# Shifting the token chunk borders to 364, 728 and 1088, and starting four streamed tensors 8 bytes into their rows

## The chip, the cores and the metric

The kernel runs on one core of one Trainium2 chip. The metric is the device time of one execution in microseconds. Before the change, three runs gave 1800.13, 1801.63 and 1802.25 us, a median of 1801.63 us. Five engines work side by side: PE (TensorE, the matmuls, with PEld for its weight loads), DVE (VectorE), ACT (ScalarE), POOL (GpSimd) and SP (SyncE, which only issues transfers).

## The reference, cut to what matters

One step of a small encoder: 1024 prompt rows and 64 sample rows of width 1024. The kernel treats them as T = 1088 tokens side by side. Layer by layer it computes

```python
h   = rmsnorm(x, g_norm1) * (1 + sc1) + sh1
z   = h @ w_in                                  # 1024 x 2464
mix = concat(mla(z), retention(z), stick_breaking(z)) @ w_o    # 1024 x 1024
x   = x + g1 * mix
h   = rmsnorm(x, g_norm2) * (1 + sc2) + sh2
a, b = split(h @ w_up)                          # 1024 x 5632, two branches of 2816
y   = (silu(causal_conv3(a)) * b) @ w_down      # 2816 x 1024
x   = x + g2 * y
out = rmsnorm(x, g_final)
```

All is float32. The sample's caches enter the attention part, which this change leaves alone.

## The kernel before, in words

The work is one program with one instruction stream for each engine, written out by hand; semaphores order the streams. The stages follow each other: transposes and the first norm, the projection `w_in` (line 1748), the mixers, then the late stages, which are what the change touches.

In the late stages the tokens lie along the free axis: a tensor `[128, KT, T]` holds 1024 features as KT = 8 rows of 128 partitions and T = 1088 tokens in each row, 4352 bytes a row. The tokens are cut into three chunks by `CHUNKS`. Chunk 0 is columns 0 to 363 (364 wide), chunk 1 columns 364 to 725 and chunk 2 columns 726 to 1087 (362 wide each).

Every large product of these stages is done in three matmuls: an operand is split into a rounded float32r part (`hi`) and the rest (`lo`), and weight_hi x hi, weight_lo x hi and weight_hi x lo are added in PSUM. The weights are the stationary side, the activations the streamed (moving) side. The streamed tensors are `a_hi` and `a_lo` (named `act_hi` and `act_lo` in the profile, 8 rows each) and `u_hi` and `u_lo` (2 rows each, one for even and one for odd tiles).

- `project(out, c, slot)` (line 1965) streams chunk c of all eight rows: 24 matmuls in a row into one PSUM bank. It serves the output projection `w_o` (24 pairs of feature tile d and chunk c, in the order of `PROJ`, each followed by one float32 matmul of line 1973 that sums squares) and both branches of `w_up`.
- `down(f, slot, ring, tile_no, n)` (line 2024) does `w_down` for one hidden tile f: 24 pieces q, each of three matmuls (u_hi, u_hi, u_lo), where q goes over d = q // 3 and c = q % 3. A part n is four pieces, 12 matmuls.
- `up(...)` makes one hidden tile of the MLP: for n = 0 to 5 it calls `project` for chunk n % 3 and branch n // 3 and then `down` part n of the tile before. There are 22 hidden tiles. `very_first` is another order for the first tile alone (both branches of a chunk one after the other, no `down`).

So one hidden tile is 6 x 24 + 72 = 216 matmuls. Each `project` and each piece of `down` waits on semaphores of ACT and DVE that empty the PSUM banks and write the streamed tensors: ACT writes `a_hi` and `u_hi` (line 1177), DVE writes `a_lo` and `u_lo` (line 1611) and adds PSUM into the residual (lines 1556 and 1620).

`NORM_RUNS` cuts the columns for the two norms; its second half is `CHUNKS`, its first half is for the early norm. `spare` is a tensor that nothing uses: its size `FF_SPARE` keeps the tensors behind it, the weights `wt_raw` and `wt_parts` first, from overlapping `mix_raw`.

Each tensor begins at a multiple of 32 bytes in its partition (in the kernel before `u_hi` at 19488, `u_lo` at 28192, `act_hi` at 115808, `act_lo` at 150624, `wt_parts` at 66656). A row of 4352 bytes is 272 times 16 bytes, so where a chunk begins within 16 bytes is the same in each row of all four tensors: chunk 0 at 0, chunk 1 (column 364, byte 1456) at 0, chunk 2 (column 726, byte 2904) at 8.

Of the kernel before, what the change touches and what calls it, by code (L numbers as in the profile page):

```python
# [15 lines left out]
F32R = mybir.dt.float32r  # L16
# [6 lines left out]
KT = D // P  # L23
LP, LS = 1024, 64
T = LP + LS
PAST = 512
NTILE = 9
ROWS = [P] * 8 + [LS]
CHUNKS = [(0, 364), (364, 726), (726, 1088)]
CW = 364  # L30
H_MLA, NOPE, ROPE, HV = 8, 64, 32, 64
QD = NOPE + ROPE
# [7 lines left out]
NF = FF // P  # L40
# [3 lines left out]
N_TAB = 11  # L44
AG = 512

NORM_RUNS = ([(0, 128), (128, 364), (364, 726), (726, 1088)], CHUNKS)
NH = (0, KT * 4)
ADA_A, ADA_G = 4, 12
MLA_SCALE = float(QD) ** -0.5  # L50
# [3 lines left out]
def segments(c):  # L54

    return split_run(*CHUNKS[c])

# [4 lines left out]

def chunk_of(t, runs=CHUNKS):

# [67 lines left out]
KINDS = [("S", 0), ("M", 0), ("M", 1), ("S", 1), ("M", 2), ("M", 3), ("S", 2), ("M", 4), ("M", 5), ("S", 3),  # L132
         ("M", 6), ("M", 7)]
UNITS = [(n, kind, h) for n in range(NTILE) for kind, h in KINDS]
FF_SPARE = KT * T - (4 * T + 2 * (T + 4) + T + 2 + 2 * CW + 8 + 4 * NF + 9)
T_LAG = {"M": 2, "S": 5}
EARLY_SPLIT = 103
MIX_STEP = 17
# [84 lines left out]
def build(nc, I, O, stop_after=None):  # L223
# [5 lines left out]
    with ctx:  # L229
# [117 lines left out]
        s4 = sbuf(late)  # L347
# [1 line left out]
        mix_scope = ExitStack()  # L349
        mix_raw = sbuf(mix_scope)("mix_raw", [KT, T])  # L350
        mix_scope.close()
        u_hi = s4("u_hi", [2, T], F32R)
        u_lo = s4("u_lo", [2, T], F32R)
        a_ext = s4("a_ext", [2, T + 4])
        conv = s4("conv", [T + 2])
        u_val = s4("u_val", [2, CW])
# [4 lines left out]
        wt_raw = s4("wt_raw", [RAW_SLOTS, KT * P])  # L361
        wt_parts = s4("wt_parts", [WT_SLOTS, 2, KT * P], F32R)
        wt_hi, wt_lo = wt_parts[:, :, 0, :], wt_parts[:, :, 1, :]
        a_hi = s4("act_hi", [KT, T], F32R)
        a_lo = s4("act_lo", [KT, T], F32R)
        res = s4("residual", [KT, T])
        late.close()

# [445 lines left out]
        def _(act):  # L814
# [36 lines left out]
            def square(c, k, j):  # L851

                a, b = CHUNKS[c]
                if j >= 2:
# [3 lines left out]
            def rstd(c):  # L858

                a, b = CHUNKS[c]  # L860
                out = norm_bufs[1]["rb"][:, a:b]
# [5 lines left out]
            def h_high(n, c):  # L867
                for k in range(KT):
                    j = NH[n] + 8 * c + k
                    act.wait_ge(s_hn, j + 1)  # L870
                    base = NORM_RUNS[n][c][0]
                    for a, b, which in split_run(*NORM_RUNS[n][c]):
                        last = act.activation(norm_bufs[n]["hi"][:, k, a:b],
# [55 lines left out]
            split_w_in(0, 0)  # L929
            for c in range(len(NORM_RUNS[0])):  # L930
                h_high(0, c)
# [190 lines left out]
            pieces_done(act, ORDER[-1])  # L1122
            for c, (lo, hi) in enumerate(CHUNKS):
                for k in (0, 4):
# [93 lines left out]
        def _(dve):  # L1218
# [73 lines left out]
            def normed(n, c, k):  # L1292
                bufs = norm_bufs[n]
                j = NH[n] + 8 * c + k
                if k == 0:
                    dve.wait_ge(s_rb, 3 * n + next(i for i, x in enumerate(CHUNKS) if NORM_RUNS[n][c][1] <= x[1]) + 1)
                if j >= 3:
                    dve.wait_ge(s_h, j - 2)
                base = NORM_RUNS[n][c][0]
                for a, b, which in split_run(*NORM_RUNS[n][c]):  # L1300
# [777 lines left out]
```

## Time and profile before

| what | value |
|---|---|
| median of three runs | 1801.63 us (1800.13 to 1802.25) |
| span of the profiled execution | 1796.0 us |
| PE busy / PEld busy | 94% / 84% of the span |
| DVE / ACT / POOL busy | 59% / 36% / 9% |
| mean granted TensorE clock | 0.963 of full |

The profile lists one time for its execution, the span from the first to the last instruction; the median of the runs is 5.6 us above it (0.3%), which is what lies around the span. The busy time of PE counts matmuls that overlap, and their ends are modelled, so a busy PE is not a PE at its peak: how long a matmul really holds the engine is read from a stretch that holds a known number of them, as its length divided by that number. This is called the pitch below.

### The profile page before, as it was taken

To read this page: it belongs to the slowest core of one execution; us is meant where nothing else is said; L and a number is where in the kernel's file an instruction comes from. 1 tells how busy PE (TensorE), PEld (TensorE's weight loads), DVE (VectorE), ACT (ScalarE), POOL (GpSimd) and SP (SyncE) were. 2 spreads that over 40 slices of the span, in tenths; PEclk is the share of its full clock that TensorE was granted. 3 is DMA by queue.
4 is the path that set the end of the run, shared out by engine and by line. 5 is a ranking of instruction groups with operands and counts; after the bars stand their busy time and mean duration, and the time that the engine had idled before them with its cause. 6 is when DMAs were issued, how large, how long until landed. Compare 5 with 4: busy or idle time off the path is not lost.

```text
span 1796.0 us, 27961 instructions
## 1 busy us (share of the span) xinstructions
PE 1680.7 (94%) x10081; PEld 1505.3 (84%) x10081; DVE 1061.4 (59%) x2259; ACT 644.5 (36%) x1242; POOL 164.6 (9%) x220
## 2 busy tenths in 40 slices
PE   6699999979789999999899899999999999999996
PEld 4499999835566677777898899999999999999996
DVE  4853333247777766766424676666656565666657
ACT  6531211125555665667413422122212222212213
POOL 0011111122322221311000000000000000000000
PEclk8799999988888899999999999999999999999999
DMA  7564444431121101005410111111111111111002
GB/s 246 179 223 153 130 131 147 126 121 36 44 88 46 46 13 46 16 1 172 151 44 12 48 48 36 59 35 47 37 56 42 40 48 46 47 35 58 12 0 113
DMA packets 114423, 133.63 MB, mean 74 GB/s; under 512 B 15003, under 2 KB 91722, under 8 KB 113002
## 3 DMA queue, kind: packets, MB, share of 16 engines
q1 hardware_dynamic: 110953, 121.83, 21.5%
q0 software_dynamic: 3328, 10.73, 1.7%
q8 instruction: 46, 0.75, 0.2%
q14 instruction: 32, 0.25, 0.0%
q10 hardware_dynamic: 64, 0.07, 0.0%
HBM read 107.54 MB, written 27.29 MB: 75 GB/s over the span
## 4 chain that ended last, share of the span: by engine, by line
PE 84%; DVE 7%; ACT 4%; issue 3%; DMA 1%; SPq 0%; DVEq 0%; ACTq 0%; POOLq 0%
PE psum L1965 33%; PE psum L2024 15%; PE psum L1748 13%; PE psum L1936 5%; PE psum L1889 3%; PE psum L1918 2%; PE psum L1833 2%; PE psum L1893 2%; PE psum L1787 1%; PE psum L1782 1%; PE psum L1814 1%; PE psum L1683 1%; PE psum L1684 1%; DVE h_lo L1313 1%; PE psum L1973 1%
## 5 line engine op out<-in xcount | busy, mean ns | idle before, releaser
L1965 PE MATMUL psum<-act_hi,wt_parts 128*128 128x362 f32 (+1 forms) x2496 | 620.1, 330 | 13.3 <-DVE act_lo L1548 5.7
L1965 PEld LDWEIGHTS psum<-act_hi,wt_parts 128*128 128x128 f32 x2496 | 442.7, 189 | 19.7 <-issue 10.7
L1620 DVE SCALAR_TENSOR_TENSOR residual<-psum,mod,residual 128x364 f32<-128x364 f32 (+2 forms) x704 | 299.9, 494 | 257.7 <-PE psum L2024 257.5
L1965 PE MATMUL psum<-act_lo,wt_parts 128*128 128x362 f32 (+1 forms) x1248 | 408.8, 328 | 0.0
L2024 PE MATMUL psum<-u_hi,wt_parts 128*128 128x362 f32 (+1 forms) x1056 | 263.3, 331 | 3.0 <-issue 3.0
L1965 PEld LDWEIGHTS psum<-act_lo,wt_parts 128*128 128x128 f32 x1248 | 235.7, 189 | 0.0
L1748 PE MATMUL psum<-w_hi,h_hi 128*128 128x308 f32 (+1 forms) x576 | 178.0, 309 | 14.1 <-DVE h_lo L1313 13.0
L2024 PEld LDWEIGHTS psum<-u_hi,wt_parts 128*128 128x128 f32 x1056 | 188.1, 189 | 3.3 <-issue 3.3
L1748 PE MATMUL psum<-w_lo,h_hi 128*128 128x308 f32 (+1 forms) x576 | 177.3, 308 | 0.0
L1748 PE MATMUL psum<-w_hi,h_lo 128*128 128x308 f32 (+1 forms) x576 | 176.8, 307 | 0.0
L2024 PE MATMUL psum<-u_lo,wt_parts 128*128 128x364 f32 (+1 forms) x528 | 174.8, 331 | 0.0
L1177 ACT ACTIVATE u_hi<-u_val 128x362 fp32r<-128x362 f32 (+1 forms) x66 | 33.4, 507 | 291.0 <-DVE u_val L1603 291.0
L1340 DVE COPY z_out<-psum 128x308 f32<-128x308 f32 (+1 forms) x72 | 34.3, 477 | 161.2 <-PE psum L1748 156.2
L1748 PEld LDWEIGHTS psum<-w_hi,h_hi 128*128 128x128 f32 (+1 forms) x576 | 107.1, 186 | 20.0 <-issue 8.8
L1156 ACT ACTIVATE a_ext<-psum 128x364 f32<-128x364 f32 (+1 forms) x88 | 32.1, 392 | 225.0 <-PE psum L1965 225.0
L1748 PEld LDWEIGHTS psum<-w_lo,h_hi 128*128 128x128 f32 (+1 forms) x576 | 107.1, 186 | 2.2
L1748 PEld LDWEIGHTS psum<-w_hi,h_lo 128*128 128x128 f32 (+1 forms) x576 | 106.8, 185 | 0.4
L1080 ACT ACTIVATE pT<-psum 128x512 f32<-128x512 f32 (+3 forms) x156 | 69.2, 475 | 100.0 <-PE psum L1918 99.9
L1936 PEld LDWEIGHTS psum<-v_mla,pT 128*128 128x128 f32 (+1 forms) x656 | 82.9, 195 | 25.5 <-issue 8.6
L1523 DVE TENSOR_TENSOR wt_parts<-wt_raw,wt_parts 128x1024 fp32r<-128x1024 f32 x74 | 91.0, 1232 | 21.6 <-ACT wt_parts L1101 21.6
L2024 PEld LDWEIGHTS psum<-u_lo,wt_parts 128*128 128x128 f32 x528 | 100.4, 190 | 0.0
L1936 PE MATMUL psum<-v_mla,pT 128*128 128x64 f32 (+1 forms) x656 | 84.6, 276 | 5.4 <-DVE mixtok L1518 2.8
(215 smaller groups left out, 2287.9 us busy)
## 6 DMA issues: line engine op xcount, KB each, us to landing
ada_raw<-in_w_ada SPq DMA_DIRECT2D x48, 512.0 KB, 4.3
wt_raw<-in_w_up SPq DMA_DIRECT2D x44, 512.0 KB, 3.8
wt_raw<-in_w_down SPq DMA_DIRECT2D x22, 512.0 KB, 4.4
w_raw<-in_w_in SPq DMA_DIRECT2D x16, 616.0 KB, 7.1
z_scratch<-z_out POOLq DMA_DIRECT2D x64, 154.0 KB, 2.3
z_in<-z_scratch SPq DMA_DIRECT2D x8, 1232.0 KB, 5.3
xT_scratch<-xT SPq DMA_DIRECT2D x1, 4352.0 KB, 16.3
residual<-xT_scratch SPq DMA_DIRECT2D x1, 4352.0 KB, 14.3
```

What stands on the lines that cost most here:

```text
L1080: last = act.activation(pT[:, wn % 4, :len(blocks), :r], src[:, :len(blocks), :r], ACT.Copy)\
L1340: dve.tensor_copy(z_out[:ROWS[t], t % 3, :], bank[t % 3][:ROWS[t], 0:ZG]).then_inc(s_zc, 1)
L1523: dve.tensor_tensor(wt_lo[:, slot], wt_raw[:, raw], wt_hi[:, slot].bitcast(F32), ALU.subtract)\
L1620: last = dve.scalar_tensor_tensor(out=res[:, d, a:b], in0=bank[4 + q % 4][:, a - CHUNKS[c][0]:b - CHUNKS[c][0]], scalar=mod[:, 40 + d, whi ...
L1748: last = pe.matmul(bank[t % 3][:r, 0:ZG], hh[:, k, P * t:P * t + r], ww[:, slot, k, :], start=(k == 0 and m == 0), stop=(k == KT - 1 and m ...
L1833: last = pe.matmul(b7[:r, 0:384], qnT[:, k, :r], w_uq[:, k, 384 * (s - 2):384 * (s - 1)], start=(k == 0), stop=(k == 2))
L1889: last = pe.matmul(out, qT[:QD, slot, h, :r], kT[:QD, h, first + a:first + b], start=True, stop=True)
L1893: last = pe.matmul(out, sqT[lo:lo + 64, slot, h // 2, :r], skT[lo:lo + 64, h // 2, first + a:first + b], start=True, stop=True)
L1918: last = pe.transpose(out[:size, P * k:P * k + r], src[:, col - first:col - first + size], ident[:r, :r])
L1936: last = pe.matmul(bank[6][:r, 64 * (v % 8):64 * (v % 8) + 64], pT[:size, W_NO[x] % 4, k % 4, :r], vals, start=(k == 0), stop=(k == len(bl ...
L1965: last = pe.matmul(out[:, :b - a], ww[:, slot, P * k:P * k + P], aa[:, k, a:b], start=(k == 0 and m == 0), stop=(k == KT - 1 and m == 2))
L2024: last = pe.matmul(bank[4 + q % 4][:, :b - a], ww[:, ring, P * d:P * d + P], uu[:, slot, a:b], start=(m == 0), stop=(m == 2))
```

## The change

The border between chunk 1 and chunk 2 goes from column 726 to 728, so the chunks are 364, 364 and 360 wide; the early norm's cut moves with it. The four streamed tensors get 8 more elements at their end, and their data begin at element 2 of what is allocated. `FF_SPARE` shrinks by 16 elements, so `wt_raw`, `wt_parts` and `act_hi` stay where they were.

```diff
-CHUNKS = [(0, 364), (364, 726), (726, 1088)]
+CHUNKS = [(0, 364), (364, 728), (728, 1088)]
...
-NORM_RUNS = ([(0, 128), (128, 364), (364, 726), (726, 1088)], CHUNKS)
+NORM_RUNS = ([(0, 128), (128, 364), (364, 728), (728, 1088)], CHUNKS)
...
-FF_SPARE = KT * T - (4 * T + 2 * (T + 4) + T + 2 + 2 * CW + 8 + 4 * NF + 9)
+OFF = 2
+FF_SPARE = KT * T - (4 * T + 16 + 2 * (T + 4) + T + 2 + 2 * CW + 8 + 4 * NF + 9)
...
-        u_hi = s4("u_hi", [2, T], F32R)
-        u_lo = s4("u_lo", [2, T], F32R)
+        def off_line(name, rows):
+            whole = s4(name, [rows * T + 8], F32R)
+            return whole[:, OFF:OFF + rows * T].rearrange("p (a n) -> p a n", a=rows)
+
+        u_hi = off_line("u_hi", 2)
+        u_lo = off_line("u_lo", 2)
...
-        a_hi = s4("act_hi", [KT, T], F32R)
-        a_lo = s4("act_lo", [KT, T], F32R)
+        a_hi = off_line("act_hi", KT)
+        a_lo = off_line("act_lo", KT)
```

After the change each chunk of each of the four tensors begins 8 bytes past a multiple of 16: columns 0, 364 and 728 are bytes 0, 1456 and 2912, all multiples of 16, and 8 is added. Nothing else of the program is edited: the instructions, their order and their semaphores are the same.

## Rows read from the trace of the kernel before

**Rows 1.** The page: busy time of PE, and the chain that ended last

```profile
PE 1680.7 (94%) x10081; PEld 1505.3 (84%) x10081; DVE 1061.4 (59%) x2259; ACT 644.5 (36%) x1242; POOL 164.6 (9%) x220
...
PE 84%; DVE 7%; ACT 4%; issue 3%; DMA 1%; SPq 0%; DVEq 0%; ACTq 0%; POOLq 0%
PE psum L1965 33%; PE psum L2024 15%; PE psum L1748 13%; PE psum L1936 5%; PE psum L1889 3%; PE psum L1918 2%; PE psum L1833 2%; PE psum L1893 2%; PE psum L1787 1%; PE psum L1782 1%; PE psum L1814 1%; PE psum L1683 1%; PE psum L1684 1%; DVE h_lo L1313 1%; PE psum L1973 1%
```

**Rows 2.** Stretches of the late stages, all engines (columns in the first line)

```profile
core 0: us, PE busy (x) PEld busy (x) DVE busy (x) ACT busy (x) POOL busy (x), PEclk, DMA share, GB/s
865.00:986.40 121.40, 119.78 (x672) 113.61 (x672) 46.82 (x74) 34.18 (x55) 0.00 (x0) 0.99 0.19 61
986.40:1022.17 35.77, 29.75 (x169) 29.49 (x169) 22.93 (x57) 19.26 (x36) 0.00 (x0) 0.95 0.19 55
1022.17:1757.00 734.83, 734.83 (x4455) 734.83 (x4455) 464.61 (x991) 165.24 (x244) 0.00 (x0) 1.00 0.13 40
```

**Rows 3.** Stretches, L1965 alone: five calls of project on chunk 0, MLP

```profile
1063.76:1067.75 4.00, 4.00 (x24) 3.85 (x24) 1.00 0.00 0
...
sum 19.98, PE 19.98 PEld 19.27; mean PE 4.00 PEld 3.85
```

**Rows 4.** Stretches, L1965 alone: five calls of project on chunk 1, MLP

```profile
1069.76:1073.72 3.96, 3.96 (x24) 3.81 (x24) 1.00 0.46 132
...
sum 19.79, PE 19.79 PEld 19.07; mean PE 3.96 PEld 3.81
```

**Rows 5.** Stretches, L1965 alone: five calls of project on chunk 2, MLP

```profile
1075.73:1079.57 3.85, 3.85 (x24) 3.72 (x24) 1.00 0.00 0
...
sum 19.23, PE 19.23 PEld 18.58; mean PE 3.85 PEld 3.72
```

**Rows 6.** A stretch, L1748 alone: 48 matmuls of the input projection, 308 wide

```profile
258.37:265.17 6.80, 6.80 (x48) 6.71 (x47) 1.00 0.41 123
```

**Rows 7.** A stretch, L1965 alone: chunk 2, both branches of the first hidden tile

```profile
1002.13:1010.21 8.07, 8.07 (x48) 8.07 (x49) 1.00 0.22 67
```

**Rows 8.** Stretches, L1965 alone: chunks 0, 1 and 2 in the output projection

```profile
892.61:896.89 4.28, 4.28 (x24) 4.02 (x24) 1.00 0.00 0
897.23:901.46 4.24, 4.24 (x24) 3.99 (x24) 1.00 0.43 123
901.79:905.99 4.20, 4.20 (x24) 3.95 (x24) 1.00 0.00 0
```

**Rows 9.** Stretches, L2024 alone: four pieces of chunk 0 in those parts

```profile
1085.57:1086.07 0.50, 0.50 (x3) 0.50 (x4) 1.00 0.00 0
...
sum 2.00, PE 2.00 PEld 1.85; mean PE 0.50 PEld 0.46
```

**Rows 10.** Stretches, L2024 alone: four pieces of chunk 2 in those parts

```profile
1086.57:1087.08 0.51, 0.51 (x4) 0.51 (x4) 1.00 0.00 0
...
sum 2.02, PE 2.02 PEld 1.88; mean PE 0.51 PEld 0.47
```

**Rows 11.** Stretches, L2024 alone: three parts of down, twelve matmuls each

```profile
1085.57:1087.58 2.01, 2.01 (x12) 1.86 (x12) 1.00 0.01 2
...
sum 6.02, PE 6.02 PEld 5.58; mean PE 2.01 PEld 1.86
```

**Rows 12.** The instructions that write u_lo on DVE and u_hi on ACT

```profile
L1611 DVE TENSOR_TENSOR u_lo<-u_val,u_hi x66: 526/530/539, 1013.4 to 1761.3; 128x362 fp32r<-128x362 f32 x44, 128x364 fp32r<-128x364 f32 x22
L1177 ACT ACTIVATE u_hi<-u_val x66: 505/507/510, 1012.9 to 1760.8; 128x362 fp32r<-128x362 f32 x44, 128x364 fp32r<-128x364 f32 x22
```

**Rows 13.** Groups by line and shape, 1022 to 1757 us (busy us, mean ns | idle before)

```profile
L1620 DVE SCALAR_TENSOR_TENSOR residual<-psum,mod,residual 128x364 f32<-128x364 f32 x167 | 98.3, 589 | 6.3 <-PE psum L2024 6.3
L1620 DVE SCALAR_TENSOR_TENSOR residual<-psum,mod,residual 128x362 f32<-128x362 f32 x167 | 98.2, 588 | 119.6 <-PE psum L2024 119.6
```

## Prediction

> **What bounds the kernel now.** I read the page's busy times and chain first. PE is busy for 94% of the span and holds 84% of the chain; the two lines of the late products, L1965 and L2024, alone hold 33% and 15% of it [rows 1]. Then the stretches by stage: from 1022 to 1757 us PE is busy in all of 734.83 us, at granted clock 1.00 (2.4 GHz), while DVE is busy 464.61 us and ACT 165.24 us [rows 2]. No engine makes PE wait there, so this stretch is as long as 4455 matmuls times their pitch, 734.83 / 4455 = 164.9 ns. The output projection before it is nearly the same: 119.78 of 121.40 us [rows 2]. Only between 986 and 1022 us does PE lose 6 us to other engines (the second norm).
>
> The reader's next question is what sets the pitch, and for that I cut the stretch by chunk. 24 matmuls of `project` are followed to the start of the next line, five times each. Chunk 0 takes 19.98 us / 120 = 166.5 ns [rows 3], chunk 1 19.79 / 120 = 164.9 ns [rows 4], chunk 2 19.23 / 120 = 160.3 ns [rows 5]. What a column costs comes from the input projection, whose 308-wide streams take 6.80 us / 48 = 141.7 ns [rows 6]: 56 columns fewer than chunk 0 and 24.8 ns less, 0.44 ns a column, so two columns are 0.9 ns. Chunks 1 and 2 have the same width and differ by 4.6 ns; what tells them apart in the code is where they start: chunk 1 at a multiple of 16 bytes, chunk 2 at 8 past one. So far it looks as if a start at 8 saved some 5 ns.
>
> Three rows spoil this picture. In the first hidden tile the same chunk 2 with the same start takes 8.07 us / 48 = 168.1 ns, of which a slow first matmul after a wait is only a small part [rows 7]. In the output projection chunk 2 is only 0.04 us in 24 (1.7 ns a matmul) better than chunk 1 and 0.08 us (3.3 ns) better than chunk 0 [rows 8]. In `down` chunk 2 is no better at all: twelve matmuls take 2.02 us, 168.3 ns, against 2.00 us, 166.7 ns, for chunk 0, which is wider [rows 9, 10]. The start at 8 thus permits the short pitch but doesn't guarantee it; it holds while equal streams follow each other in long rows.
>
> **The change part by part.** Every estimate is a difference of pitches times a count. 22 hidden tiles x 2 branches x 24 = 1056 `project` matmuls a chunk; `w_o` has 8 calls a chunk; `down` 22 x 72 = 1584 matmuls. The sum is made against the profiled span, 1796.0 us, and carried to the median of the runs, 5.6 us above it, unchanged.
>
> *The MLP's project, chunks 0 and 1 (364 wide, start 0 becomes 8).* Best end: chunk 2's 160.3 ns and two columns more, 161.2 ns: 5.3 and 3.7 ns gained, 1056 x 9.0 = 9.5 us. Least end that still has an effect: what the start is worth in the output projection, 3.3 ns against chunk 0 less 0.9 ns of width, so 166.5 - 2.4 = 164.1 ns. I take the middle, 162.6 ns, because [rows 3 to 5] and [rows 8] show the same two starts in two surroundings and nothing says which the new streams will be nearer: 3.9 and 2.3 ns, 4.1 + 2.4 = 6.5 us gained. The other end, a loss, is that chunk 1 takes chunk 0's pitch with its width: 1.6 x 1056 = 1.7 us.
>
> *Chunk 2 (362 becomes 360 wide, still at 8).* Two columns, 0.9 ns x 1056 = 1.0 us gained, if it keeps its short pitch. If it falls back to what it had in the first tile, near 166.5 ns, it loses 6.2 x 1056 = 6.5 us; that is the upper end.
>
> *The output projection.* Chunks 0 and 1 to about 4.22 us (chunk 2's 4.20 and two columns in 24 matmuls), chunk 2 to 4.18: 0.06, 0.02 and 0.02 us x 8 = 0.8 us gained; at worst 0.04 and 0.08 us lost on chunks 1 and 2, 1.0 us.
>
> *`down`.* Now 6.02 us / 36 = 167.2 ns [rows 11]; the widths' sum stays 1088. Best end: chunk 2's 160.3 ns for the mean width, 160.6 ns, 6.6 x 1584 = 10.5 us gained, because all streams would now start alike, where before each third piece differed. Worst end: chunks 0 and 1 as chunk 2 is now, 1.6 ns x 1056 = 1.7 us lost. I take 0, the value nearest to [rows 9, 10], where the start at 8 shows no gain in threes.
>
> *The writers and readers.* ACT and DVE write the shifted tensors with starts at 8; chunk 2 was written so before, and the 66 instructions of each kind lie within 505 to 510 and 526 to 539 ns [rows 12]. DVE's adds take 589 ns at 364 and 588 ns at 362 columns [rows 13]. Both engines have over a third of the stretch free, which hides a few ns; without that cover, the roughly 30 instructions a tile would cost some 0.1 us a tile. No wait, instruction, queue or transfer is added. A faster PE asks more of DVE: 464.61 us of work in perhaps 715 us is still no bound. The early norm and the second norm get two columns more in one chunk and two fewer in the next: nothing.
>
> Sum: 6.5 + 1.0 + 0.8 + 0 = 8.3 us. Span 1787.7 us, and the median 1793.3 us.
>
> Here a rule is weighed. The rows above show that pitch isn't a matter of width alone. The Trainium skill, "TensorE: Matmul & The Clock Gate", section "Back-to-back issue gap", gives N / 2.4 + 2.5 ns between warm matmuls, a figure in which no address stands. By it the change, which keeps 1088 columns, would be worth 0 us. Chunks 1 and 2 differ by 4.6 ns at one width, so this trace does not agree with it.
>
> **The rivals.**
>
> *All streams lock at the short pitch, `down` too.* 9.5 + 1.0 + 0.8 + 10.5 = 21.8 us: 1779.8 us. For it: chunk 2 has its short pitch in each of the five calls cut, one like the other [rows 5]; after the change no stream has another start. Against it: [rows 7, 10]. Chance 0.15.
>
> *The pitch goes by width and history, and the start is chance.* Chunk 1 becomes 364 wide and takes chunk 0's 166.5 ns: 1.7 us and 0.3 us (output projection) lost; chunk 2 gains 1.1 us; the rest stays. 1802.5 us, no change to be seen. The same comes out if the shift does nothing. For it: two columns more go with 1.6 ns more from chunk 1 to chunk 0. Against it: chunk 2 against chunk 1. Chance 0.25.
>
> *A stream pays by the 16-byte lines that it touches.* A 364-wide stream from 8 covers 92 of them instead of 91; chunk 2 keeps 91. If a line costs what its four columns do, 1.8 ns, then 2 x (1056 + 192 + 528) = 3552 matmuls lose 6.4 us: 1808.0 us. Against it: before the change all three chunks cover 91 lines, and their pitches lie 6.2 ns apart [rows 3, 5]. Chance 0.04. The Trainium skill, "SBUF — State Buffer", section "Specifications (TRN2)", names lines of 16 bytes and a penalty for each crossing to a new one; this trace shows no such penalty at an uneven start.
>
> *Slower: chunk 2 loses its short pitch.* The place is `project` on chunk 2. Before, hi and lo streams lay a multiple of 64 bytes apart; the 8 extra elements put `act_lo` 32 bytes further, so the third matmul of each three now starts elsewhere within 64 bytes than the two before it, and the even sequence of [rows 5] is broken. Then chunk 2 takes about 166.5 ns (6.5 us lost), chunk 1 as in the width rival 2.0 us, the output projection's chunk 2 0.6 us: 9.1 us, 1810.7 us. It decides as soon as chunk 2 loses more than chunks 0 and 1 gain: from a pitch of 160.3 + 6.5 / 1.056 = 166.5 ns if they gain as forecast, from 160.3 ns on if they gain nothing. For it: [rows 7]. Chance 0.19.
>
> **How the numbers follow.** The forecast, 1793.3 us, has chance 0.37, with its own range 1786 to 1799 (project at 161.2 or at 164.1 ns, `down` some us either way). What a measurement of this kernel can tell from no change is 0.2%, 3.6 us. Faster: the full lock's 0.15 and 0.34 of the forecast, 0.49. Within: the forecast's other 0.03 and 0.23 of the width rival, 0.26. Slower: 0.19, 0.04 by lines and 0.02 of the width rival, 0.25. The range 1779 to 1808 leaves out half of the loss on chunk 2 and of the loss by lines, and the cases beyond a full lock: 2 in 10 at most.
>
> **What would show it.** Stretches of 24 `project` matmuls in the MLP: near 162 ns for chunks 0 and 1 and 159 to 160 ns for chunk 2 by the forecast, 166.5 for both 364-wide chunks by the width rival, 166 for chunk 2 by the slower one. Twelve matmuls of `down`: 2.00 us by the forecast, 1.93 us if all lock. The forecast is wrong if a chunk's pitch goes up, if `down` moves by over 2 ns a matmul, or if PE gets idle time between 1022 and 1757 us.

## The result and the profile after

The changed kernel takes 1810.47 us (median of four runs, 1808.89 to 1812.60) against 1800.88 us before (four runs): a ratio of 1.0063 with a 95% interval of 1.0049 to 1.0077. The forecast was a gain of 8.3 us; it became a loss of some 10 us.

The page after, busy times and chain, answers to [rows 1]:

```profile
PE 1691.9 (93%) x10081; PEld 1515.7 (84%) x10081; DVE 1060.3 (59%) x2259; ACT 643.9 (36%) x1242; POOL 164.3 (9%) x220
...
PE 84%; DVE 7%; ACT 4%; issue 3%; DMA 1%; SPq 0%; DVEq 0%; ACTq 0%; POOLq 0%
```

PE is busy 11.2 us longer with the same 10081 matmuls; DVE, ACT and POOL are as they were, and the chain has the same shares. The loss is thus in the matmuls themselves. The stretches by stage of the kernel after answer to [rows 2]:

```profile
core 0: us, PE busy (x) PEld busy (x) DVE busy (x) ACT busy (x) POOL busy (x), PEclk, DMA share, GB/s
865.50:989.50 124.00, 121.42 (x672) 115.29 (x672) 47.99 (x76) 34.93 (x56) 0.00 (x0) 0.99 0.18 61
989.50:1025.80 36.30, 31.49 (x169) 31.22 (x170) 21.84 (x55) 18.61 (x35) 0.00 (x0) 0.91 0.19 55
1025.80:1771.20 745.40, 745.40 (x4454) 745.40 (x4454) 464.19 (x991) 165.22 (x244) 0.00 (x0) 1.00 0.13 39
```

The MLP stretch takes 745.40 us against 734.83, with PE busy in all of it at granted clock 1.00 in both: 10.6 us lost without one idle moment. The output projection loses 2.6 us, the second norm 0.5 us; all ahead of 865 us differs by 0.5 us, all behind the MLP by 0.1. These add up to the 14.3 us between the two profiled spans (1810.3 and 1796.0). The medians are only 9.6 us apart, with an interval of 8.8 to 13.9 us. Not all of the 5.6 us between span and median of the kernel before lie around the span: around that of the changed kernel there are 1.6 us (1811.94 and 1810.3). The execution profiled before was thus some 4 us shorter than its median one.

Such differences lie outside the MLP. Five traces hold the code of before: its own and those of four later runs (e5, e6, e12 and e16) that only add matmuls behind the last output. In them the first `project` starts between 862.7 and 868.9 us, but from the first `down` to the end of the last `project` they all take 734.56 us. The same stretch in before, in e16_full_map and in the changed kernel:

```profile
1022.17:1756.73 734.56, 734.56 (x4453) 734.56 (x4453) 464.61 (x991) 165.24 (x244) 0.00 (x0) 1.00 0.13 40
...
1025.80:1760.36 734.56, 734.56 (x4454) 734.56 (x4453) 464.62 (x991) 165.33 (x244) 0.00 (x0) 1.00 0.13 40
...
1025.79:1771.05 745.26, 745.26 (x4453) 745.26 (x4453) 464.19 (x991) 165.22 (x244) 0.00 (x0) 1.00 0.13 39
```

The change costs 10.7 us here, whichever execution is profiled. The experiments below are compared by this stretch too; it tells apart what the medians, with their intervals of 0.13 to 0.23% either way, can't.

Five calls of `project` on chunk 0, on chunk 1 and on chunk 2 of the kernel after, answering to [rows 3 to 5], first call and sum of each:

```profile
1104.10:1108.10 4.00, 4.00 (x24) 3.86 (x24) 1.00 0.00 0
...
sum 20.02, PE 20.02 PEld 19.30; mean PE 4.00 PEld 3.86
...
1092.03:1096.06 4.03, 4.03 (x24) 3.89 (x24) 1.00 0.82 255
...
sum 20.16, PE 20.16 PEld 19.45; mean PE 4.03 PEld 3.89
...
1098.09:1102.10 4.01, 4.01 (x24) 3.87 (x24) 1.00 0.00 0
...
sum 20.04, PE 20.04 PEld 19.35; mean PE 4.01 PEld 3.87
```

Divided by 120: 166.8, 168.0 and 167.0 ns, where [rows 3 to 5] gave 166.5, 164.9 and 160.3 (160.2 over all steady calls, the value used below). The chunk that became narrower lost most. Three parts of `down`, answering to [rows 11], and chunks 0, 1 and 2 of the output projection, answering to [rows 8]:

```profile
1096.06:1098.09 2.02, 2.02 (x12) 1.87 (x12) 1.00 0.05 14
...
sum 6.04, PE 6.04 PEld 5.60; mean PE 2.01 PEld 1.87
...
893.50:897.80 4.29, 4.29 (x24) 4.03 (x24) 1.00 0.00 0
898.13:902.50 4.38, 4.38 (x24) 4.11 (x24) 1.00 0.41 119
902.84:907.10 4.27, 4.27 (x24) 4.01 (x24) 1.00 0.00 0
```

`down` is 0.5 ns a matmul worse, the output projection 0.22 us in each round of three calls.

### The profile page after: what moved, and what is told of

Its sections match the earlier page's. It is cut to its first block, busy times and chain, and to the rows that moved or that the text cites. A ratio compares the mean times of both kernels' runs of the same rounds, so it can differ in the third digit from the quotient of the medians.

```text
span 1810.3 us, 27961 instructions
## 1 busy us (share of the span) xinstructions
PE 1691.9 (93%) x10081; PEld 1515.7 (84%) x10081; DVE 1060.3 (59%) x2259; ACT 643.9 (36%) x1242; POOL 164.3 (9%) x220
## 4 chain that ended last, share of the span: by engine, by line
PE 84%; DVE 7%; ACT 4%; issue 3%; DMA 1%; SPq 0%; DVEq 0%; ACTq 0%; POOLq 0%
PE psum L1970 33%; PE psum L2029 15%; PE psum L1753 13%; PE psum L1941 5%; PE psum L1894 3%; PE psum L1923 2%; PE psum L1838 2%; PE psum L1898 2%; PE psum L1792 1%; PE psum L1787 1%; PE psum L1819 1%; PE psum L1688 1%; PE psum L1689 1%; DVE h_lo L1318 1%; PE psum L1978 1%
## 5 line engine op out<-in xcount | busy, mean ns | idle before, releaser
L1970 PE MATMUL psum<-act_hi,wt_parts 128*128 128x364 f32 (+1 forms) x2496 | 630.5, 334 | 13.0 <-DVE act_lo L1553 5.7
L1970 PEld LDWEIGHTS psum<-act_hi,wt_parts 128*128 128x128 f32 x2496 | 449.0, 191 | 19.4 <-issue 10.4
L1625 DVE SCALAR_TENSOR_TENSOR residual<-psum,mod,residual 128x364 f32<-128x364 f32 (+1 forms) x704 | 299.5, 495 | 268.9 <-PE psum L2029 268.9
L1970 PE MATMUL psum<-act_lo,wt_parts 128*128 128x364 f32 (+1 forms) x1248 | 413.0, 331 | 0.0
L2029 PE MATMUL psum<-u_hi,wt_parts 128*128 128x364 f32 (+1 forms) x1056 | 262.6, 330 | 3.0 <-issue 3.0
L1182 ACT ACTIVATE u_hi<-u_val 128x364 fp32r<-128x364 f32 (+1 forms) x66 | 33.5, 508 | 296.4 <-DVE u_val L1608 296.4
L1345 DVE COPY z_out<-psum 128x308 f32<-128x308 f32 (+1 forms) x72 | 34.3, 477 | 160.2 <-PE psum L1753 158.3
```

The source lines that it names most:

```text
L1345: dve.tensor_copy(z_out[:ROWS[t], t % 3, :], bank[t % 3][:ROWS[t], 0:ZG]).then_inc(s_zc, 1)
L1625: last = dve.scalar_tensor_tensor(out=res[:, d, a:b], in0=bank[4 + q % 4][:, a - CHUNKS[c][0]:b - CHUNKS[c][0]], scalar=mod[:, 40 + d, whi ...
L1970: last = pe.matmul(out[:, :b - a], ww[:, slot, P * k:P * k + P], aa[:, k, a:b], start=(k == 0 and m == 0), stop=(k == KT - 1 and m == 2))
L2029: last = pe.matmul(bank[4 + q % 4][:, :b - a], ww[:, ring, P * d:P * d + P], uu[:, slot, a:b], start=(m == 0), stop=(m == 2))
```

## The experiments

In this section a start is given as an element: how many 4-byte columns it lies past the old beginning of the `act` tensors, modulo 64, that is, within 256 bytes. A row of 1088 columns is 4352 bytes, 17 times 256, so all rows of a tensor start alike in this measure. Before, the chunks were 364 wide at element 0, 362 at 44 and 362 at 22 (written 364@0, 362@44, 362@22); after, 364@2, 364@46 and 360@26. "lo +8" says that the lo tensor lies 8 elements further within 256 bytes than the hi tensor; in the kernel before they lie alike (`act_lo` - `act_hi` = 34816 = 136 x 256 bytes), in the changed one lo is at +8.

The pitches below are read as those above: steady calls of `project` in the MLP, the mean of the two branches, and parts of `down`, in ns a matmul. The stretch is that from the first `down` to the end of the last `project`, in us.

| kernel | chunk 0 | chunk 1 | chunk 2 | down | stretch | ratio to before [95%] |
|---|---|---|---|---|---|---|
| before | 166.5 | 164.9 | 160.2 | 167.3 | 734.6 | 1 |
| after | 166.8 | 168.0 | 167.0 | 167.7 | 745.3 | 1.0063 [1.0049, 1.0077] |
| e1_same_64 | 166.7 | 166.7 | 165.3 | 167.2 | 741.5 | 1.0046 [1.0031, 1.0061] |
| e2_chunks_only | 166.6 | 166.0 | 166.7 | 167.1 | 741.9 | 1.0044 [1.0027, 1.0060] |
| e3_shift_only | 167.0 | 166.8 | 166.5 | 167.0 | 742.8 | 1.0042 [1.0023, 1.0061] |
| e4_pad_only | 166.6 | 165.0 | 164.3 | 166.8 | 738.2 | 1.0025 [1.0010, 1.0040] |
| e7_u_only | 166.6 | 165.1 | 163.5 | 166.9 | 737.6 | 1.0025 [1.0012, 1.0038] |
| e8_a_only | 166.4 | 164.8 | 166.7 | 166.6 | 739.9 | 1.0029 [1.0015, 1.0043] |
| e9_starts | 167.5 | 166.4 | 165.5 | 165.8 | 740.0 | 1.0031 [1.0019, 1.0044] |
| e10_starts_rows | 167.2 | 165.1 | 165.7 | 164.4 | 736.6 | 1.0005 [0.9990, 1.0020] |
| e11_rows_only | 166.4 | 164.4 | 162.0 | 166.4 | 734.5 | 1.0009 [0.9993, 1.0025] |
| e13_starts_256 | 163.4 | 161.1 | 160.9 | 164.9 | 725.1 | 0.9923 [0.9900, 0.9946] |
| e14_change_256 | 166.7 | 167.7 | 166.6 | 166.6 | 742.8 | 1.0040 [1.0025, 1.0056] |
| e15_pad_256 | 166.5 | 164.9 | 160.2 | 167.3 | 734.6 | 0.9992 [0.9977, 1.0006] |
| e17_starts_no_rows | 163.9 | 162.2 | 161.7 | 165.6 | 728.5 | 0.9925 [0.9906, 0.9944] |
| e18_best | 165.1 | 160.9 | 161.1 | 163.5 | 724.5 | 0.9936 [0.9923, 0.9950] |

### The parts of the change, one at a time

**e1_same_64** is the changed kernel with 16 pad elements in place of 8, so that hi and lo lie alike within 64 bytes.

```diff
-            whole = s4(name, [rows * T + 8], F32R)
+            whole = s4(name, [rows * T + 16], F32R)
```

> The changed kernel with 16 elements of padding in each of the four tensors instead of 8, so that hi and lo streams of a chunk again start at the same place within 64 bytes; starts at 8 past a multiple of 16 and chunks 364, 364, 360 as changed. Theory A (the short pitch needs hi and lo streams that start alike within 64 bytes; the 32-byte step between them broke it): chunk 2 goes back from 167 to about 160 ns a matmul in the MLP's project, chunks 0 and 1 to 161 to 166.5 ns, total 1803 us or less. Theory B (width and history set the pitch, the relation does not matter): 167 to 168 ns in all chunks as in the changed kernel, total about 1810 us.

Chunk 2 took 165.3 ns, 1.7 ns back of 6.8, and chunk 1 166.7 ns, 1.3 back of 3.1; the stretch got back 3.8 us of 10.7. Either the relation of hi and lo is only part of the cause, or 64 bytes are not the measure.

**e2_chunks_only** is the kernel before with the border at 728 and no tensor moved.

```diff
-CHUNKS = [(0, 364), (364, 726), (726, 1088)]
+CHUNKS = [(0, 364), (364, 728), (728, 1088)]
```

> The kernel before with only the chunk border moved to 728; no shift, no padding. All three chunks start at a multiple of 16 bytes, hi and lo alike. Theory A (relation of hi and lo): no loss by a broken relation, chunk 0 at 166.5 ns, chunk 1 at 166.5 ns with its new width, chunk 2 between 159 and 164 ns, total 1800 to 1804 us. Theory C (the start at 8 of the old chunk 2 is what gave the short pitch): chunk 2 goes to about 165 ns, total about 1808 us.

**e3_shift_only** is the changed kernel with the border back at 726.

```diff
-CHUNKS = [(0, 364), (364, 728), (728, 1088)]
+CHUNKS = [(0, 364), (364, 726), (726, 1088)]
```

> The changed kernel with the old chunk border at 726: only the 8-byte shift and the 8 elements of padding. Chunks 0 and 1 start at 8 past a multiple of 16, chunk 2 at a multiple of 16; lo streams lie 32 bytes further within 64 than hi streams. Theory A: all chunks at 166 to 168 ns, total about 1810 us. Theory C: chunks 0 and 1 fall to about 161 ns and chunk 2 rises to 165 ns, total about 1796 us.

Each half of the change takes the short pitch from chunk 2 by itself. Chunk 2 in e2_chunks_only, with hi and lo alike, 360 wide (first call and sum of five):

```profile
1094.59:1098.59 4.00, 4.00 (x24) 3.86 (x24) 1.00 0.00 0
...
sum 20.00, PE 20.00 PEld 19.28; mean PE 4.00 PEld 3.86
```

166.7 ns with nothing moved but the border. That ends the rival by lines too: here all chunks start at a multiple of 16 bytes and touch 91, 91 and 90 lines of 16, one fewer than before, and chunk 2 is 6.5 ns slower. The Trainium skill, "SBUF — State Buffer", section "Specifications (TRN2)", names a penalty for each crossing to a new 16-byte line; in this run one line fewer went with 6.5 ns more. That e2 and e3 add up to more than the whole change is no riddle: both count the loss of chunk 2.

**e4_pad_only** is the kernel before with the 8 extra elements at each tensor's end and no shift: only lo moves, by 32 bytes.

```diff
-OFF = 2
+OFF = 0
```

> The kernel before with only the 8 elements of padding in each of the four tensors: chunks and starts within 16 bytes as before, but lo streams lie 32 bytes further within 64 than hi streams. Theory A: chunk 2 loses its 160 ns and goes to 165 to 167 ns, total about 1808 us. Theories B and C: nothing changes, chunk 2 at 160 ns, total 1801 us.

Chunk 2 rose to 164.3 ns, chunks 0 and 1 stayed. The relation of hi and lo has a price of its own, 4.1 ns x 1056 = 4.3 us; the ratio of 1.0025 (4.5 us) and the stretch (3.6 us more, with 0.5 ns a matmul gained in `down`) agree. The lo tensor of `u` moved too, but in e16_full_map below rows of 362@22 with lo +8, where no `down` runs, take 164.4 to 164.8 ns as well. The relation explains part of the loss in a kernel whose chunk 2 is 362@22, not why e2 loses.

### Which starts are short

**e5_map** adds to the kernel before, behind its last output, rows of 33 matmuls like those of `project`, whose results go nowhere, for many widths and starts. Its time and those of the other maps mean nothing.

```diff
+CASES = [(n, s, lo) for lo in (0, 8) for n in (362, 364, 360, 358, 366, 368) for s in range(0, 16, 2)]
...
+            for case in CASES:
+                stream(*case)
```

> The kernel before, and behind its last output 131 rows of 33 more matmuls each, with nothing else running: project's pattern (weights hi, lo, hi; streams hi, hi, lo over the eight rows) at widths 358 to 368 and all even starts within 64 bytes, with lo streams alike or 32 bytes further, and some other widths. The results of these matmuls go nowhere. Theory D (the pitch belongs to the pair of width and start within 64 bytes, whatever ran before and runs beside): 364 from element 0 takes 166.5 ns, 362 from element 12 takes 164.9 ns, 362 from element 6 takes 160.2 ns, and the map shows which other pairs have the short pitch. Theory E (the short pitch comes from what ran before or runs beside, so that one pair has several pitches): 362 from element 6 takes 163 to 167 ns in some of its repeats behind other widths of the transpose ahead of it, and a start has no clear order. Theory A: each pair is faster with lo alike than with lo 32 bytes further.

Rows of e5_map, 320, 352, 384 and 512 wide at element 0: each stretch goes from the start of the 9th matmul to that of the 33rd, which is 24 pitches (the count includes matmuls that reach into it).

```profile
2363.72:2367.24 3.52, 3.52 (x25) 3.42 (x25) 1.00 0.00 0
...
2426.03:2429.88 3.84, 3.84 (x26) 3.84 (x25) 1.00 0.00 0
2447.82:2451.98 4.16, 4.16 (x25) 4.16 (x26) 1.00 0.00 0
2499.27:2504.71 5.44, 5.44 (x24) 4.25 (x23) 1.00 0.00 0
```

146.7, 160.0, 173.3 and 226.7 ns. In these four rows a column costs 1 / 2.4 ns and 13.3 ns lie on top. That is no rule for all: at element 0 too, 308 columns took 140.1 ns, 1.6 under this line, and 448 took 202.5, 2.5 over it; 320 and 512 columns at element 6 took 149.4 and 233.3. The Trainium skill, "TensorE: Matmul & The Clock Gate", section "Back-to-back issue gap", has N / 2.4 + 2.5 ns, which it calls the gap of an isolated matmul; these rows have 13.3 in place of its 2.5. Widths near 362 moved with the start by 5 ns and more, and one case (362 at element 6) gave 166.7 or 161.7 by what ran ahead of it: a start has more than one steady pitch.

**e6_entry_map** has the same rows, each with six different matmuls (96 to 110 columns) just ahead of it, for the 8 even starts below element 16 at 362, 364 and 360 columns.

```diff
+CASES = [(n, s, lo, 33, g) for n, lo in ((362, 0), (364, 0), (360, 0), (362, 8)) for s in range(0, 16, 2)
+         for g in (96, 98, 102, 104, 106, 110)]
```

> The kernel before, and behind its last output rows of 33 more matmuls in project's pattern as in the map, each row entered six times behind one other matmul of 96, 98, 102, 104, 106 or 110 columns, so that only the moment of entry differs. Results go nowhere. Theory E (a row of equal streams settles on one of a few pitches, by the moment at which it is entered): a pair of width and start shows two or more of 160.0, 163.3 and 166.7 ns over its six entries; 362 wide reaches 160 in some, 364 wide stays at 166.7 nearly always. Theory D (pitch belongs to width and start alone): the six entries of a pair agree within 0.5 ns. Theory C (starts at 8 past a multiple of 16 are better): starts 2, 6, 10, 14 have clearly lower means than 0, 4, 8, 12 at each width.

362@4 took 160.0 ns from all six entries, and 362@8 166.7 from all six:

```profile
1872.87:1876.71 3.84, 3.84 (x26) 3.84 (x25) 1.00 0.01 4
...
1899.94:1903.78 3.84, 3.84 (x26) 3.84 (x25) 1.00 0.00 0
1938.41:1942.41 4.00, 4.00 (x26) 4.00 (x25) 1.00 0.00 0
...
1966.46:1970.46 4.00, 4.00 (x26) 4.00 (x25) 1.00 0.00 0
```

Both starts are multiples of 16 bytes, so the place within 16 bytes, by which the prediction told chunk 1 from chunk 2, does not tell a short pitch from a long one. Starts 8 past 16 (elements 2, 6, 10, 14) took 165.0 (160.0 once), 161.7 or 166.7, 164.4, and 160.0 or 166.7. 364 was 166.7 in most rows (168.3 at 8, 168.9 in four of six at 6, 163.3 in five of six at 10, 162.2 in two of six at 12), 360 between 163.3 and 166.7 and never 160.

**e7_u_only** and **e8_a_only** shift one pair of tensors alone, with 16 pad elements and the old border: the first moves what `down` streams, the second what `project` streams. In e7 (in e8 the other two lines stay):

```diff
-        a_hi = off_line("act_hi", KT)
-        a_lo = off_line("act_lo", KT)
+        a_hi = s4("act_hi", [KT, T], F32R)
+        a_lo = s4("act_lo", [KT, T], F32R)
```

> The kernel before with u_hi and u_lo alone shifted by 8 bytes (16 elements of padding, hi and lo alike within 64 bytes); project's streams a_hi and a_lo keep width, start and address. Theory E: what runs between the calls of project changes the entry, and chunk 2 of project can leave 160 ns (to 163 to 167) although its own streams are untouched; total up to 1806 us. Theory D: project's three pitches stay at 166.5, 164.9 and 160.2 ns, only down moves, by under 1 ns; total 1799 to 1801 us.

> The kernel before with a_hi and a_lo alone shifted by 8 bytes (16 elements of padding, hi and lo alike within 64 bytes); down's streams keep their addresses. Chunks 0 and 1 start at 8 past a multiple of 16, chunk 2 at a multiple of 16. Theory C: chunks 0 and 1 fall to 161 ns, chunk 2 rises to 165 ns, total about 1792 us. Theory E: chunk 0 (364 wide) stays near 166.7 ns, chunks 1 and 2 (362 wide) land somewhere between 160 and 166.7 ns, total 1796 to 1806 us.

In e7 the streams of `project` are untouched, yet chunk 2 went from 160.2 to 163.5 ns: how `down` runs ahead of it changes what it settles at. In e8 chunk 2 went to 166.7. So both the streams and the entry count; e7 left the question whether entry is all.

**e9_starts** gives the chunks starts from e6's list (elements 10, 4 and 4 modulo 16), in rows of 1120 columns with gaps, at the old widths. **e10_starts_rows** also puts `down` in an order by chunk for every tile, **e11_rows_only** that order alone.

```diff
+AT = (10, 388, 756)
+TW = 1120
...
-    return (q % KT, q // KT) if isinstance(f, int) and f == NF - 1 else divmod(q, 3)
+    return q % KT, q // KT
```

> The kernel before with its widths 364, 362, 362, but rows of the four tensors spread to 1120 columns so that every stream of a chunk, hi and lo, begins where the entry map showed its shortest pitch: chunk 0 at element 10 within 64 bytes (counted from the old start), chunks 1 and 2 at element 4. Theory F (a row of equal streams has the pitch that its width, its start within 64 bytes and the likeness of hi and lo allow; starts 8 past 16 have no worth of their own): chunk 0 at 163.3 ns, chunks 1 and 2 at 160.0 ns in the MLP's project, down within 1 ns of 167, total about 8 us under the kernel before. Theory E alone (entry decides): no such order, each chunk anywhere between 160 and 167 ns, total within 5 us of before.

> The same, and the pieces of down are taken chunk by chunk in all hidden tiles (eight feature tiles of one chunk after another), so that the twelve matmuls of a part stream one chunk. Theory F: down's pitch falls from 167 to 161 to 163 ns too, 6 to 9 us more, total about 15 us under the kernel before. If waits and switches of PSUM bank after every third matmul are what costs in down: its pitch stays near 167 ns and the total is that of the kernel with the starts alone.

> The kernel before with down taken chunk by chunk and nothing else changed. Theory F: down at 164 to 166 ns, its chunks near what project has at the same starts (166.5, 164.9, 160 to 165 ns), total 2 to 5 us less, if chunk 2 of project keeps its 160 ns; by theory E its entry changes and it may leave it, which costs up to 6 us. If the switches after every third matmul cost: down at 167 ns.

None of the three is faster than before: chunk 2 took 165.5 and 165.7 ns at a start that was firm by its place within 16 elements, and the order by chunk alone is worth nothing (1.0009). What that start left out: column 756 is element 52 of 64, not 4, and rows of 1120 columns are 17.5 times 256 bytes. In e11, whose streams of `project` are those of before, chunk 2 took 160.2 ns in one branch and 163.7 in the other: the entry once more.

**e12_addr_map** takes 362@4 and changes one address at a time: lo by 8 to 128 elements, the start by 16 to 112, the row's length by 16 to 64, the weights.

```diff
+CASES = [(362, 4, lo, 33, g, T, P) for lo in (0, 8, 16, 32, 48, 64, 128) for g in G]
+CASES += [(362, 4 + 16 * j, 0, 33, g, T, P) for j in range(1, 8) for g in G]
+CASES += [(362, 4, 0, 33, g, T + x, P) for x in (16, 32, 48, 64) for g in G]
```

> The kernel before, and behind its last output 35 further groups of rows of 33 matmuls (three entries each, as in the entry map): 362 wide from element 4, which gave 160.0 ns in all its entries, with lo streams 8 to 128 elements further, with the whole start moved by multiples of 16 elements, with rows 16 to 64 elements longer; and widths 360, 362, 364 with all eight rows at one address, or all weights at one address. Results go nowhere. Theory G (what counts is how a stream's address lies to the one before it within more than 64 bytes, 256 perhaps): 160.0 ns stays with lo 64 or 128 elements further and with rows 64 longer, and is lost with 16, 32, 48. Theory F (64 bytes are all that counts): 160.0 ns stays with every multiple of 16 elements and is lost with 8 alone. If the weights' addresses matter: the rows with one weight address differ from the entry map's.

Rows of e12_addr_map in this order: lo alike; lo +8; lo +64; start 20; start 68; rows 16 columns longer; rows 64 longer:

```profile
1813.24:1817.09 3.84, 3.84 (x26) 3.84 (x25) 1.00 0.02 4
...
1829.60:1833.55 3.95, 3.95 (x26) 3.95 (x25) 1.00 0.00 0
...
1896.39:1900.23 3.84, 3.84 (x26) 3.84 (x25) 1.00 0.02 4
...
1928.95:1932.87 3.92, 3.92 (x27) 3.92 (x26) 1.00 0.00 0
...
1978.68:1982.52 3.84, 3.84 (x26) 3.84 (x25) 1.00 0.02 4
...
2044.89:2048.84 3.96, 3.96 (x26) 3.96 (x25) 1.00 0.00 0
...
2094.84:2098.68 3.84, 3.84 (x25) 3.84 (x24) 1.00 0.00 0
```

160.0, 164.7, 160.0, 163.3, 160.0, 164.8 and 160.0 ns. Lo, start and row length all return to 160.0 ns from every entry at 64 elements, 256 bytes, and at no smaller step that was tried (start 36 had it from one entry of three; start 52 took 165.5). Starts 84, 100 and 116 gave the pitches of 20, 36 and 52 again. Taking all eight rows of a tensor from one address, or all weights from one address, left the pitches as in e6. That is why e1 and e8, alike within 64 bytes only, and e9 and e10, with rows of 17.5 x 256 bytes, could not settle what hi and lo and the starts are worth.

### With 256 bytes as the measure

**e13_starts_256** is e10 with rows of `act` 1152 columns long (18 x 256 bytes) and chunks at elements 10, 4 and 4. **e17_starts_no_rows** is e13 with the old order of `down`. **e18_best** gives the `u` tensors such rows too, with chunks at the places in 256 bytes that are elements 10, 4 and 46 of `act`.

```diff
+AT = {KT: (10, 388, 772), 2: (10, 388, 756)}
+TW = 1120
...
+                self.tile = s4(name, [rows, TW if rows == 2 else 1152], F32R)
```

> The kernel with chosen starts and down by chunks once more, with rows of the a tensors 1152 columns long (a multiple of 256 bytes, as before the change) instead of 1120, and chunks at elements 10, 4, 4 within 256 bytes. Theory G: project's chunks 1 and 2 go to 160.0 ns and chunk 0 to 163 to 167 ns, down near 164 ns; total 6 to 10 us under the kernel before. Theory F alone: no difference to the kernel with 1120 columns, 165 to 167 ns.

> The kernel with 1152-column rows and chosen starts, but with down in its old order. Theory G: project keeps 163.5, 161 and 161 ns, down goes back to about 167 ns, 3 to 4 us more than with down by chunks, total still 7 to 12 us under the kernel before. If down by chunks was what gave project its good entries: project at 163 to 166 ns and the total near that of the kernel before.

> The kernel with 1152-column rows for a, chosen starts and down by chunks, and now the u tensors too have rows of 1152 columns and starts that lie at elements 10, 4 and 46 within 256 bytes counted as in the map (where 364 columns gave 163.3 and 362 columns 160.0 ns). Theory G: down falls from 165 to 161 to 163 ns, another 3 to 5 us, total 1777 to 1783 us, some 18 to 22 us under the kernel before. If down's waits and PSUM switches after every third matmul keep it at 165 ns: total as with the a tensors alone, about 1785 us.

e13 takes 1785.48 us, 0.77% under the kernel before, with the widths and the matmuls of before; e17 takes 0.75% less. The medians can't part the two, but the stretch can: e13 gains 9.4 us in it and e17 6.0, so the starts bring most of it, and the order of `down`, worth nothing alone (e11), brings 3.4 us with them. e18 gains 10.1 us there: its parts of `down` are shortest, 163.5 ns, but its chunk 0 is 165.1. Chunk 1 of e13 in `project` (first of five, sum), then the stretch that answers to [rows 2], and the stretch of the table for e17:

```profile
1081.16:1085.02 3.86, 3.86 (x24) 3.73 (x24) 1.00 0.83 260
...
sum 19.32, PE 19.32 PEld 18.67; mean PE 3.86 PEld 3.73
...
1016.40:1742.00 725.60, 725.60 (x4457) 725.60 (x4456) 465.62 (x989) 165.25 (x244) 0.00 (x0) 1.00 0.13 40
...
1019.59:1748.12 728.53, 728.53 (x4454) 728.53 (x4453) 464.29 (x991) 165.27 (x244) 0.00 (x0) 1.00 0.13 40
```

161.0 ns where before had 164.9, and 9.2 us less for the stretch of [rows 2], PE busy throughout as before. Of the 15.0 us between the two profiled spans (1781.0 and 1796.0), 4.1 lie ahead of the first `project`, where nothing was edited and executions of the code of before differ by 6 us. What the new starts are worth is thus nearer to 11 us than to the 15.2 between the medians; the interval, 9.7 to 18.0 us, holds both.

**e14_change_256** is the changed kernel with 64 pad elements, so that hi and lo are alike within 256 bytes; **e15_pad_256** is the kernel before with the same pad and no shift.

```diff
-            whole = s4(name, [rows * T + 8], F32R)
+            whole = s4(name, [rows * T + 64], F32R)
```

> The changed kernel with 64 elements of padding in each of the four tensors instead of 8: hi and lo streams of a chunk start alike within 256 bytes; starts at 8 past a multiple of 16 and widths 364, 364, 360 as changed. Theory G: the loss by the broken relation goes, 1 to 2 ns on chunk 1; what remains is the loss by widths and starts, all chunks at 166.7 ns as in the entry map, total about 1805 us. Theory A in full: chunk 2 returns to 160 ns.

> The kernel before with 64 elements of padding in each of the four tensors, no shift, old border. Theory G: hi and lo alike within 256 bytes as before, so project keeps 166.5, 164.9 and 160.2 ns, total as before; with 8 elements of padding chunk 2 had gone to 164.3 ns. Theory E alone (any small change of what runs between moves the entry): chunk 2 may leave 160 ns here too.

e15 moves every lo tensor by 256 bytes and gives the pitches of before to about a hundredth of a ns. Chunk 2 of e15, first call and sum of five, beside [rows 5]:

```profile
1095.98:1099.82 3.85, 3.85 (x24) 3.71 (x24) 1.00 0.00 0
...
sum 19.23, PE 19.23 PEld 18.58; mean PE 3.85 PEld 3.72
```

So moving tensors is not itself a loss, and the idea that any edit shuffles the entry falls. e14 takes away the hi and lo difference where it counts. Its chunks 1 and 2, sums of five:

```profile
sum 20.12, PE 20.12 PEld 19.39; mean PE 4.03 PEld 3.88
...
sum 19.98, PE 19.98 PEld 19.27; mean PE 4.00 PEld 3.85
```

167.7 and 166.6 ns: 0.3 and 0.5 ns of 3.1 and 6.8 came back in `project`, 1.1 ns in `down` (1.7 us). The intervals of the ratios, 1.0040 and 1.0063, overlap, but in the stretch 8.3 of the 10.7 us stay: the larger part of the loss is not due to hi and lo.

**e16_full_map** runs the widths and starts of before, after and e2 in rows by themselves, and 362 and 364 at all even starts within 256 bytes.

```diff
+KEPT = [(364, 0), (362, 44), (362, 22)]
+CHANGED = [(364, 2), (364, 46), (360, 26)]
+BORDER = [(364, 44), (360, 24)]
```

> The kernel before, and behind its last output rows of 33 matmuls by themselves for the very widths and starts within 256 bytes that the kernels have: before (364 at element 0, 362 at 44, 362 at 22), changed (364 at 2, 364 at 46, 360 at 26), border alone (364 at 44, 360 at 24), each with lo alike and lo 8 elements further; and all even starts of 256 bytes for 362 and 364 columns with two entries each. Results go nowhere. Theory G (width, start and lo's offset within 256 bytes set the pitch): the pairs of the kernel before give 166.7, 165 and 160 to 164 ns with lo alike, those of the changed kernel 166.7, 167 to 169 and 166 to 167 ns with lo 8 further, and with lo alike no less than 166 ns. Otherwise, if surroundings matter more: the changed pairs come out below 165 ns here.

Rows of e16_full_map: 364@0; 362@44; 362@22 with three entries; then with lo +8 364@2, 364@46 and 360@26:

```profile
1816.79:1820.79 4.00, 4.00 (x26) 4.00 (x25) 1.00 0.01 4
...
1850.39:1854.34 3.95, 3.95 (x26) 3.95 (x26) 1.00 0.00 0
...
1878.15:1882.15 4.00, 4.00 (x27) 4.00 (x26) 1.00 0.01 4
1883.70:1887.55 3.84, 3.84 (x25) 3.84 (x25) 1.00 0.00 0
1889.13:1893.06 3.92, 3.92 (x26) 3.92 (x25) 1.00 0.00 0
...
1928.14:1932.14 4.00, 4.00 (x26) 4.00 (x25) 1.00 0.00 0
...
1967.66:1971.71 4.05, 4.05 (x26) 4.05 (x25) 1.00 0.00 0
...
2001.43:2005.43 4.00, 4.00 (x26) 4.00 (x25) 1.00 0.00 0
```

Alone, behind the last output, with DVE, ACT and POOL idle and transfers next to none (DMA share 0.00 to 0.02), they show what they show in the kernels: 166.7 and 164.5 ns for chunks 0 and 1 of before (166.5, 164.9 in the kernel); for the changed chunks 166.7, 168.8 and 166.7 (166.8, 168.0, 167.0); for chunks 1 and 2 of e2, 364@44 and 360@24, 165.8 and 166.7 (166.0, 166.7). So neither transfers nor the other engines are needed for the long pitches. Old chunk 2, 362@22, has three steady pitches, 166.7, 160.0 and 163.3, by what ran ahead. The kernel before happens to enter it at 160.2; e7, with another `down` ahead, at 163.5. With lo +8 the map gives it 164.4 to 164.8; e4 had 164.3. Hi and lo alike is not always better: 360@24 took 164.5 ns with lo +8. Of the 32 even starts, 362 took 160.0 from both entries tried at elements 4, 28, 34, 46 and 48 alone; 364 took 162.2 at best. Over these rows the starts 8 past 16 average 164.3 ns at 362 columns and 167.2 at 364, the multiples of 16 average 164.4 and 165.8: as a class they gain nothing.

The three pitches of 362@22 are in the kernel before as well, if each call is read from its 9th matmul to its 24th, 15 pitches: a call on chunk 2 in the MLP, one in the output projection, and the second one of the first hidden tile:

```profile
1077.01:1079.41 2.40, 2.40 (x17) 2.40 (x16) 1.00 0.00 0
903.38:905.83 2.45, 2.45 (x16) 2.45 (x16) 1.00 0.00 0
1007.54:1010.04 2.50, 2.50 (x16) 2.50 (x16) 1.00 0.00 0
```

160.0, 163.3 and 166.7 ns.

## Why the prediction was wrong

The reading of the bound held: the MLP stretch is matmuls times pitch, and nothing but the pitch moved it. So did four smaller points: no engine but PE matters, the writers and adds cost nothing, the rule without addresses and the rival by 16-byte lines are both wrong. Its own first sign of being wrong, a chunk whose pitch goes up, came on all three chunks. The failure is in the terms for the pitch, by 1056 matmuls a chunk:

| step | forecast | measured |
|---|---|---|
| project, chunk 0 | -3.9 ns, -4.1 us | +0.4 ns, +0.4 us |
| project, chunk 1 | -2.3 ns, -2.4 us | +3.1 ns, +3.2 us |
| project, chunk 2 | -0.9 ns, -1.0 us | +6.8 ns, +7.2 us |
| output projection | -0.8 us | +1.8 us in its calls |
| `down` | 0 | +0.4 ns, +0.6 us |
| sum | -8.3 us | +13.2 us of 14.3 between the spans |

The step that failed is "what tells them apart in the code is where they start: chunk 1 at a multiple of 16 bytes, chunk 2 at 8 past one". Chunks 1 and 2 do differ by their start, but the class "8 past 16" was made up from few samples, elements 0 and 44 of 64 against element 22. The first term, "start 0 becomes 8", took a class where only a list exists: 364@0 and 364@2 are both 166.7, 364@46, 167.5 to 170.0 in e16, is worse than either.

The second failure is "two columns, 0.9 ns x 1056 = 1.0 us gained, if it keeps its short pitch". The 0.44 ns a column was read over 56 columns; near 362 the start is worth more than two columns (160.0 to 168.9 ns at 362 in e16, 162.2 to 173.3 at 364), and 360@24 and 360@26 take 166.7. The condition was written down, with [rows 7] against it. [Rows 7, 8] hold two further pitches of the same stream, 166.7 and 163.3 ns as read above; the trace of before alone could have told that the 160.2 ns were one state of several, and the loss deserved more than a chance of 0.19.

The slower rival's time, 1810.7 us, is near the measured one, and its place, chunk 2 of `project` at 166.5 ns, is right. Its mechanism is not: the 32 bytes between hi and lo can take the short pitch from old chunk 2 (e4), but with hi and lo alike most of the loss stays (e14, e2). That its total came near is luck: its 9.1 us stand beside 9.6 between the medians, but beside 13.2 in the terms of the table: chunk 1 (3.2 us) and the output projection (1.8 us) lost more than it had. The width rival had chunk 1 go to chunk 0's pitch; it went past it.

What stays open: why a width and a start have the pitches they have, and what in the entry picks one (the single matmul put ahead of a row is not all of it: behind 96 and 102 columns, 362@22 took 166.7 and 160.0 ns in one place of e16 and 163.3 twice in another). The runs list the pitches; none explains them. `down` doesn't follow the list either. By their addresses its streams in before are 364@48, 362@28 and 362@6, which take 166.7, 160.0 and 161.7 or 166.7 in rows, but its parts take 167.3 ns, and 166.4 when taken chunk by chunk (e11); no run tells whether the changes of bank after each third matmul, the waits or the entry do that.

## What to carry to other kernels

Where PE is never idle, the pitch of equal float32r streams is worth reading for each width and start, and two starts are no rule: measure a list of starts over a whole period (here 256 bytes) in one run before moving a tensor. With hi and lo, and the rows of a tensor, a multiple of 256 bytes apart, a row of matmuls repeats one start and the list applies to it; then choose widths and starts that keep their pitch whatever ran ahead. Here that took 9.4 us out of the MLP stretch (e13) and 6.0 with the old order of `down` (e17), without one matmul fewer. A pitch that is short in one place and long in another at the same width and start is a sign of several steady states, and an edit beside it can lose it.

## What the runs showed that was not expected

- The pitch repeats with the address of the stream modulo 256 bytes: 160.0, 163.3, 160.0 ns at starts 4, 20, 68; lo and the row's length the same. Taking all weights from one address changed nothing.
- Rows of 320, 352, 384 and 512 columns at element 0 took 146.7, 160.0, 173.3 and 226.7 ns, 13.3 ns above the columns' own time at 2.4 GHz; 308 and 448 columns do not fit.
- One start can have several steady pitches over 24 matmuls: 362@22 had 160.0, 163.3 and 166.7 ns, in a map and within the kernel before.
- A stretch of 4453 matmuls in which PE never waits took 734.56 us in each of five executions, while what lies ahead of it differed by 6 us.
- At element 0 the pitch goes with the width in uneven steps: 352, 354 and 356 columns took 160.0 ns, 358 took 163.3, 360 and 362 took 164.5, 364 took 166.7.
